# Hybrid decoder block on one core: an early combine for both token tiles, and the last half of the output scaled on GpSimd and ScalarE

## The reference

```python
logits = hf @ router_w + router_b            # 256 tokens, 32 experts
top_logits, top_idx = top_k(logits, 4); gates = softmax(top_logits)
for each expert e, on the rows that chose it:
    gu = xb @ w_gate_up[e] + b_gate_up[e]    # (1024, 2048)
    act = (clip(up, -7, 7) + 1) * min(gate, 7) * sigmoid(1.702 * min(gate, 7))
    y = act @ w_down[e] + b_down[e]          # (1024, 1024)
    out[token] += y * gates
x = x + out
return x * rsqrt(mean(x * x) + 1e-6) * final_norm_g
```

## Time and profile before

| | before |
|---|---|
| runs | 1171.4, 1170.69, 1170.59 us; median 1170.69 |
| the profiled execution: its own time | 1170.47 us |
| its span, first to last instruction | 1168.8 us (1.7 us of the time lie around it) |
| TensorE matmul busy | 1098.4 us (94%), granted clock 0.984 |
| VectorE, ScalarE, GpSimd busy | 339.9, 167.5, 3.9 us |
| read from HBM, written | 433.95 MB, 1.05 MB |

### The profile page before, as it was taken

How to read it: one execution, slowest core, us unless ns; L and a number is a source line. 1 busy time by engine, 2 the same in 40 slices (tenths; PEclk the granted TensorE clock), 3 DMA queues, 4 the chain that set the end, 5 groups by cost and what they waited for, 6 DMA issues and landing times.

```text
span 1168.8 us, 14160 instructions
## 1 busy us (share of the span) xinstructions
PE 1098.4 (94%) x5949; PEld 528.6 (45%) x5949; DVE 339.9 (29%) x739; ACT 167.5 (14%) x275; POOL 3.9 (0%) x22
## 2 busy tenths in 40 slices
PE   9999999999999999989898989898989898989897
PEld 8988884863434333333333333333333333333332
DVE  5792334462121222231213131313131313121213
ACT  3521235340000001010101010101010101010002
POOL 1000000000000000000000000000000000000000
PEclk9999999999999999999899999999999999989999
DMA  9842314869999999999999999999999999999995
GB/s 342 308 144 78 140 72 118 359 229 424 430 428 427 426 429 430 432 426 434 426 434 426 435 426 436 426 436 426 436 426 436 426 436 426 435 425 435 423 425 237
DMA packets 39622, 435.67 MB, mean 373 GB/s; under 512 B 5893, under 2 KB 5978, under 8 KB 20410
## 3 DMA queue, kind: packets, MB, share of 16 engines
q1 hardware_dynamic: 37658, 433.67, 88.4%
q10 hardware_dynamic: 1920, 1.34, 0.6%
HBM read 433.95 MB, written 1.05 MB: 372 GB/s over the span
## 4 chain that ended last, share of the span: by engine, by line
PE 59%; DMA 37%; DVE 1%; ACT 1%; SPq 1%; issue 1%; DVEq 0%; PEldq 0%
DMA ring<-in_w_down 36%; PE ps L2134 19%; PE ps L2087 14%; PE ps L1740 4%; PE ps L1596 4%; PE ps L2149 3%; PE ps L1686 3%; PE ps L1578 2%; PE ps L1736 2%; PE ps L1789 2%; PE ps L2056 2%; PE ps L1892 1%; PE ps L1936 1%; PE ps L2075 1%; DMA work<-in_mem 0%
## 5 line engine op out<-in xcount | busy, mean ns | idle before, releaser
L2134 PE MATMUL ps<-ring,work 128*64 128x512 f32 x1024 | 246.0, 630 | 40.0 <-DMA ring<-in_w_down 37.0
L2087 PE MATMUL ps<-ring,work 128*64 128x512 f32 x1024 | 225.6, 593 | 8.2 <-DMA ring<-in_w_gate_up 8.2
L2087 PE MATMUL ps<-work 128*64 128x512 f32 x1024 | 230.5, 592 | 0.0
L2134 PEld LDWEIGHTS ps<-ring,work 128*64 128x64 f32 x1024 | 80.6, 144 | 180.2 <-issue 162.6
L2087 PEld LDWEIGHTS ps<-ring,work 128*64 128x64 f32 x1024 | 71.3, 137 | 158.0 <-issue 141.3
L2087 PEld LDWEIGHTS ps<-work 128*64 128x64 f32 x1024 | 71.6, 137 | 136.3 <-issue 129.5
L1450 DVE TENSOR_SCALAR work<-ps 128x512 f32<-128x512 f32 x32 | 22.0, 687 | 196.7 <-PE ps L1578 196.7
L1473 DVE COPY work<-ps 128x512 f32<-128x512 f32 x16 | 11.1, 692 | 223.4 <-PE ps L1578 223.4
L1485 DVE COPY work<-ps 128x512 f32<-128x512 f32 (+1 forms) x16 | 11.1, 692 | 222.3 <-PE ps L2134 222.3
L2149 PE MATMUL ps<-work 128*128 128x512 f32 (+1 forms) x132 | 59.7, 608 | 10.4 <-ACT work L809 10.2
L802 ACT ACTIVATE ps<-work 128x512 f32<-128x512 f32 x32 | 19.2, 602 | 341.3 <-DVE work L1450 341.3
(11 more groups left out here) (247 smaller groups left out, 746.2 us busy)
## 6 DMA issues: line engine op xcount, KB each, us to landing
work<-in_w_gate_up SPq DMA_DIRECT2D x64, 2048.0 KB, 36.6
ring<-in_w_gate_up SPq DMA_DIRECT2D x22, 4096.0 KB, 32.2
ring<-in_w_down SPq DMA_DIRECT2D x22, 4096.0 KB, 36.3
ring<-in_w_gate_up SPq DMA_DIRECT2D x20, 2048.0 KB, 22.3
ring<-in_w_down SPq DMA_DIRECT2D x17, 2048.0 KB, 20.6
ring<-in_w_in SPq DMA_DIRECT2D x6, 2048.0 KB, 18.4
ring<-in_xattn_w_kv SPq DMA_DIRECT2D x2, 2048.0 KB, 14.5
ring<-in_w_out SPq DMA_DIRECT2D x2, 2048.0 KB, 8.0
```

What stands on the lines that cost most here:

```text
L2087: last = nc.tensor.matmul(bank(b)[p], xg_T[k][:, kb, :], quad_columns(w[:, kk, D_MODEL * (q // 2):D_MODEL * (q // 2 + 1)], q % 2), start=F ...
L2134: last = nc.tensor.matmul(bank(Y_BANK + y)[p], act_T[k][:, b, HALF * c:HALF * c + HALF], w[:, b, 512 * q:512 * q + 512], start=False, stop ...
```

## The change

Four edits:

1. In the last pair, expert n (the first of the two) is combined for both tiles, four calls of 64 rows, between `down(1, 0)` and `down(1, 1)`. What follows `down(1, 1)` is four calls of 64 rows for expert m.
2. `scaled(1, ...)` is two instructions of 512 columns, with `half_mean(0, 3)` between them. SyncE's store of tile 1 waits for both.
3. Columns 512 to 1023 of tile 0 are multiplied by the gain on GpSimd (a new `tensor_tensor`, 128 x 512, both inputs in SBUF), then by the inverse root on ScalarE (a copy with a scale), and stored from ScalarE's queue. VectorE scales columns 0 to 511 alone. GpSimd waits for all four `x3_half` (both halves of both tiles added), ScalarE for GpSimd and for the inverse.
4. The semaphores of GpSimd's early masks (`w_ba_zeroed`, `tri_ready`, `causal_ready`, `before_ready`) become one counter, `pool_masks`, in the order of its instructions.

```diff
+        last_gained = extra[6][:, D_MODEL:D_MODEL + 512]
...
-                    sp.wait_ge(S("w_ba_zeroed"), 1)
+                    sp.wait_ge(S("pool_masks"), 1)
...
-            sp.wait_ge(S("out_ready"), 1)
+            sp.wait_ge(S("out_ready"), 2)
             sp.dma_start(out[0, P:2 * P, :], x_sb[:, 1, :]).then_inc(S("out_stored"), 16)
-            for h in range(2):
-                sp.wait_ge(S("out_ready"), h + 2)
-                sp.dma_start(out[0, 0:P, 512 * h:512 * h + 512], half_of(0, h)).then_inc(S("out_stored"), 16)
+            sp.wait_ge(S("out_ready"), 3)
+            sp.dma_start(out[0, 0:P, 0:512], half_of(0, 0)).then_inc(S("out_stored"), 16)
             sp.wait_ge(S("out_stored"), 16 * 3)
...
+            pool.wait_ge(S("final_gain_loaded"), 16)
+            pool.wait_ge(S("x3_half"), 4)
+            nc.gpsimd.tensor_tensor(last_gained, half_of(0, 1), final_gain[:, 512:], ALU.mult) \
+                .then_inc(S("last_gained"), 1)
...
             tile_root(0, 2, 4)
+            act.wait_ge(S("last_gained"), 1)
+            act.wait_ge(S("x3_inverted"), 1)
+            nc.scalar.activation(half_of(0, 1), last_gained, ACT.Copy, scale=by_tile(rstd, 0)) \
+                .then_inc(S("last_scaled"), 1)
+            act.wait_ge(S("last_scaled"), 1)
+            act.dma_start(out[0, 0:P, 512:], half_of(0, 1)).then_inc(S("out_stored"), 16)
...
             invert(rstd[:, 1:2], "x3_root", 1)
+            scaled(1, slice(0, 512))
             half_mean(0, 3)
-            scaled(1, slice(0, D_MODEL))
-            invert(rstd[:, 0:1], "x3_root", 2)
+            scaled(1, slice(512, D_MODEL))
+            v.wait_ge(S("x3_root"), 2)
+            nc.vector.reciprocal(rstd[:, 0:1], rstd[:, 0:1]).then_inc(S("x3_inverted"), 1)
+            v.wait_ge(S("x3_inverted"), 1)
             scaled(0, slice(0, 512))
-            scaled(0, slice(512, D_MODEL))
...
                 down(1, 0, chunk, turned16, pieces)
+                if final:
+
+                    pe.wait_ge(S("y_early"), 2 * r + 2)
+                    for t in (1, 0):
+                        combine(t, 0, low, True, False).then_inc(S("combine_begun"), 1)
+                        combine(t, 1, high, True, False).then_inc(S("combine_begun"), 1)
                 s = down(1, 1, chunk, turned16, pieces)
                 down_done(m, s)
-
                 if final:
-
-                    pe.wait_ge(S("y_early"), 2 * r + 2)
-                    combine(1, 0, low, True, False)
-                    combine(1, 1, high, True, False).then_inc(S("combine_begun"), 1)
-                    pe.wait_ge(S("combine_begun"), r + 1)
+                    pe.wait_ge(S("combine_begun"), 4 * (r + 1))
                 for t in (1, 0):
-                    parts = ((0, high), (1, low)) if final and t == 1 else ((0, slice(0, P)), (1, slice(0, P)))
-                    for q, rows in parts:
+                    for q, rows in ((0, high), (1, low)) if final else ((0, slice(0, P)), (1, slice(0, P))):
                         if t == 1:
                             pe.wait_ge(S("y_ready" if q else "y0_ready"), before + 2)
-                        last = combine(t, q, rows, not (final and t == 1), True)
+                        last = combine(t, q, rows, not final, True)
                     last.then_inc(S("combine_filled"), 1)
```

More of the change, by code:

```diff
@@ L546, in _ @@
             nc.gpsimd.iota(p_col, pattern=[[0, 1]], base=0, channel_multiplier=1).then_inc(S("iotas_ready"), 1)
-            nc.gpsimd.memset(w_ba, 0.0).then_inc(S("w_ba_zeroed"), 1)
+            nc.gpsimd.memset(w_ba, 0.0).then_inc(S("pool_masks"), 1)
             own(pool, nc.gpsimd.memset(tri, 1.0), "pool_step")
             nc.gpsimd.affine_select(out=tri, in_=tri, compare_op=ALU.is_ge, fill=0.0, base=0,
-                                    pattern=[[1, P]], channel_multiplier=-1).then_inc(S("tri_ready"), 1)
+                                    pattern=[[1, P]], channel_multiplier=-1).then_inc(S("pool_masks"), 1)
             own(pool, nc.gpsimd.memset(causal, 0.0), "pool_step")
@@ L557, in _ @@
                                         fill=NEG, base=0, pattern=[[-1, P]], channel_multiplier=1) \
-                    .then_inc(S("causal_ready"), 1)
+                    .then_inc(S("pool_masks"), 1)
             nc.gpsimd.iota(iota_s, pattern=[[1, SLOTS]], base=1, channel_multiplier=0,
@@ L562, in _ @@
             nc.gpsimd.affine_select(out=before, in_=before, compare_op=ALU.is_gt, fill=0.0, base=0,
-                                    pattern=[[1, P]], channel_multiplier=-1).then_inc(S("before_ready"), 1)
-            nc.gpsimd.memset(ones, 1.0).then_inc(S("before_ready"), 1)
+                                    pattern=[[1, P]], channel_multiplier=-1).then_inc(S("pool_masks"), 1)
+            nc.gpsimd.memset(ones, 1.0).then_inc(S("pool_masks"), 1)
             drained(pool, "moba_oT")
@@ L1080, in _ @@
             nc.vector.transpose(flat(inv), flat(inv_T)).then_inc(S("solved"), 1)
-            v.wait_ge(S("tri_ready"), 1)
+            v.wait_ge(S("pool_masks"), 2)
             step(nc.vector.tensor_tensor(decay_T, decay_T, tri.unsqueeze(1).to_broadcast([P, 8, P]), ALU.mult))
@@ L1086, in _ @@
             token_sums("tok_q", q_square, slice(8, 16))
-            v.wait_ge(S("causal_ready"), 2)
+            v.wait_ge(S("pool_masks"), 4)
             def query_scales():
@@ L1691, in decay_sums @@
             def decay_sums():
-                pe.wait_ge(S("tri_ready"), 1)
+                pe.wait_ge(S("pool_masks"), 2)
                 take(pe, "cum_g")
@@ L2012, in _ @@
             keep_turning(12)
-            pe.wait_ge(S("before_ready"), 2)
+            pe.wait_ge(S("pool_masks"), 6)
             pe.wait_ge(S("chosen_ready"), TILES)
```

## The result

The changed kernel takes 1173.54 us in the median of 21 runs, the one before 1171.10 in 21 runs made beside it. The ratio is 1.0017, with a 95% interval of 1.0011 to 1.0023: 2.0 us slower, 1.3 to 2.7. The interval leaves out no change at all, and the 2.4 us of the forecast lie in it. The two medians alone are of less use. The times lie in two groups, clearly so after the change (ten runs up to 1172.90, eleven from 1173.54 on) and less clearly before (ten up to 1170.78, eleven from 1171.10 on). A median of 21 stands at the lower edge of the upper group, and the two edges lie 2.4 us apart; the medians of like groups lie 1.8 apart. (Against the 1172.9 of the forecast the median is 0.6 higher, inside its range; the kernel before had 1170.69 in its first three runs and 1171.10 in 21.)

The account below looks back on a forecast made before the run. With the last weight piece just in time, TensorE, then VectorE with ScalarE, then the stores set the end. Terms 1.5 - 0.2 + 1.15 = +2.4 us on the profiled 1170.47 gave 1172.9, range 1171.0 to 1173.9.

Parts of the forecast that it names:

- Edit 1 on TensorE: Early combine ahead of `down(1, 1)`: four passes and three shape changes cost TensorE 2.05 us, bounds 1.72 and 2.3.
- Behind it: After `down(1, 1)`: with expert n's calls moved away, the first add follows the down matmuls 0.54 us sooner.
- T: Time of VectorE's first add after the last combine, 1159.53 before; forecast +1.5 us, bounds +1.2 and +1.8.
- Tile 0's shorter combine: Last combine: tile 0 done 0.8 us after T, not 1.9; VectorE's work on tile 1 leaves 0.21 us usable.
- Edit 3, the meeting: GpSimd's 1.2 us product and VectorE's first `scaled(1)` exclude each other at the end; VectorE stalls 1.15 us.
- two signs: First `scaled` ending only after GpSimd's product means a real stall; taking 0.75 us beside it means no meeting.
- Rival (a): VectorE's two halves run first, GpSimd's product only behind them, delaying tile 0: +1.8 us, 1172.3; chance 0.15.
- Stores: Output stores: last landing 4.0 us behind tile 1's issue, set by issue and bytes; earlier last half gains nothing.
- Sum: Whole change: 1.5 - 0.2 + 1.15 = +2.4 us against the profiled 1170.47, so 1172.9.
- (b): Rival: GpSimd's product and VectorE's scaling both run at full speed, +1.3 us, 1171.8; chance 0.20.
- (c): Rival: late last weight piece lets early combine fill a TensorE hole; 1169.7 without stall, 1170.9 with; chance 0.07.
- (d): Rival: GpSimd's product takes far longer than 1.2 us or needs setup; at 2.2 us, 1173.9; chance 0.08.

Follow-up runs that it names:

- e1: Kernel before with only the early combine of expert n for both tiles (edit 1); ratio to before 1.0014 (1.0004 to 1.0023).
- e12: The same kernel as e1, run again; single run, span ends 20.1 us after the start of `down(1, 0)` (18.9 before).
- e6: Kernel before with only tile 1's two early combine calls ahead of `down(1, 1)`; single run, span ends 19.4 us after the start of `down(1, 0)`.
- e3: Kernel before with only tile 1 scaled in two instructions (edit 2), stored as before; ratio to before 1.0003 (0.9993 to 1.0013).
- e5: Changed kernel with a GpSimd fill of the same area in place of its product; single run, span ends 20.1 us after the start of `down(1, 0)`.
- e10: Changed kernel with GpSimd's product made twice in one instruction; single run, span ends 22.1 us after the start of `down(1, 0)`.
- e4: Changed kernel with GpSimd's product started only after VectorE's last scaling; single run, span ends 21.1 us after the start of `down(1, 0)`.
- e8: Kernel before with tile 1 scaled in two halves and the output in four stores of 256 KB; ratio to before 0.9998 (0.9989 to 1.0007).
- e9: Kernel before with GpSimd multiplying tile 1 by the gain during VectorE's adds of tile 0; ratio to before 0.9999 (0.9990 to 1.0008).
- e11: e9 with `half_mean(0, 3)` first, tile 1 scaled in two halves and the four stores of e8; ratio to before 0.9999 (0.9990 to 1.0008).

## Why the prediction was right, and where it was off

*Edit 1 on TensorE*: forecast 2.05 us ahead of `down(1, 1)` (its terms, 1.72 + 0.3, make 2.02), measured 2.1 (e1, e12, after); half of the calls cost 1.2 (e6). The bounds of 1.72, with no change of shape paid, and of 2.3, with 0.53 us a pass, were not met. *Behind it*: 0.54 back, measured 0.58 (T is 1.92 behind the down matmuls, 2.50 before). T comes 1.5 us later, as forecast, and for the reasons given.

*Tile 0's shorter combine*: only 0.2 us of it usable, since VectorE is busy with tile 1. Tile 1's store is issued at T + 4.60 in e1 and e12 against 4.82. That is the whole 0.2 us that the forecast counts under edit 2; edit 2 alone moves it by 0.02 (e3).

*Edit 3, the meeting*: right in kind, off in order and in size. The forecast had GpSimd start at T + 3.02 and VectorE at T + 3.09, and the first half wait. VectorE was first, at T + 2.99, since an add starts while `half_mean` is still in its last 0.08 us, which the working had in sequence. GpSimd came 0.07 us behind it, at T + 3.06: it began 0.17 us after the last add, where the working had 0.05. It slipped in between the halves, and the second half waited. So neither of the two signs that the forecast named came as written: the first `scaled` took 0.75 us beside the product's record, and yet there was a stall. Rival (a), where GpSimd gets in only behind both halves, was not it either: of the two, the one that had waited came next. The stall is 0.94 us, not 1.15: the product keeps VectorE out for 1.12 us from the end of its first half (its 1.2 was nearly right), and the last 0.55 us of the waiting instruction are shorter than its 0.74 alone. Tile 1's store came at T + 5.44, not 5.77.

*Stores*: forecast last landing 4.0 us behind tile 1's issue. The store from ScalarE's queue, issued 0.89 behind it, took 3.1 us in e5 and 3.2 in the changed kernel, which makes 4.0 and 4.1; before it was 4.0. (The span ends some 0.4 us later.) An earlier last half gains nothing: shown, by e5.

*Sum*: forecast +2.4, measured +2.1 from the start of `down(1, 0)` and 2.0 (1.3 to 2.7) by the ratio. What is missing, 0.3 us, lies in tile 1's store, 0.62 later against T than before in place of 0.95: 0.21 is the stall, and 0.12 is that without a stall the store would have stood at T + 4.50 (e5), not 4.62. The number alone proves little, as +2.1 lies midway between the forecast's +2.4 and the +1.8 of rival (a); it is the traces that decide between them. Which engine came first hung on 0.07 us. The forecast had the order the wrong way round, and for the right order, in rival (a), it had another outcome; that the sum still comes within 0.3 us is in part luck.

*The rivals*: (b), no meeting, is out by the changed kernel's own 1.69 us, and by e10; (c), a late last piece, by e1 and e6; (d), a longer product or a setup, by e4's 1.26 us. The low end of the range, held for (b) and (c), wasn't needed.

## What to carry to other kernels

Before work is moved ahead of a wait, look whether the wait still has a hole in it: here 14 pairs had waited for weights and the last one didn't, so the moved calls cost all they took, 2.1 us, and gave back only the 0.6 that their old place had cost. Before GpSimd is given part of a product, look at what VectorE reads in that moment: here they ran side by side when VectorE added from PSUM and one SBUF operand, and took turns when it scaled from two SBUF operands, and the waiting one's record looks like a slow instruction. And where the bytes of the stores set the end, an earlier issue of the last part gains nothing (e5). An earlier issue of the first part can (0.5 us in e8), but in e9 and e11 the stores took longer and it gained nothing either.

## What the runs showed of the hardware

- The wait of some 3 us for weights before 1087 us is followed by a stretch at 1.2 GHz in thirteen of the fourteen traces, and its length differs between programs that are alike up to there: the 16 down records behind it took 5.35 us in nine traces, 5.00 and 5.20 in e3 and e9, and 6.50 and 6.53 in two (e6 and the changed kernel). In e5 the granted clock stayed at 1.00 through it, and they took 3.65. That gained nothing, since TensorE then waited for the next weights until 1096.9, as its chain shows: the last pair began at 1149.92, as in the kernel before. So up to 5.35 us the loads hide it, and 6.5 us moves a single time by 1.2 us, more than several of the effects studied here. T, counted from a point behind it, agrees to 0.1 us among all traces with the same combine.

```profile
1063.37 33.49 DMA ring<-in_w_down
1096.86 0.14 issue
1096.99 7.10 PE ps L2146 x32
```

- An interruption of the down matmuls (64-column weights) by combine calls (64-row weights) cost about 0.36 us beyond the calls' own passes of 0.43, whether there were two passes or four: the down matmuls ended 1.22 us later in e6 and 2.08 in e1 and e12. The chain shows 1.06 and 1.92 us of it between the two stretches of down matmuls.
- GpSimd's float32 product of 128 x 512 takes 1.26 us by itself (e4), and 1.08 more for 512 further columns (e10).
- A store of 512 KB took from 2.6 us to 3.5 from issue to landing; with one and the same kernel it took 3.3 in one execution (e1) and 2.7 in another (e12).
